# The head of a one-core hybrid trunk, taken in two halves of the channels

## The reference, cut to what matters

```python
m = jax.nn.silu(cvec) @ P['ada_w'][i] + P['ada_b'][i]
sh1, sc1, g1, sh2, sc2, g2 = jnp.split(m[:, None, :].astype(x.dtype), N_MOD, axis=-1)
h = rmsnorm(x, P['norm_mix_g'][i]) * (1 + sc1) + sh1
...
u = h @ P['ssd_w_in'][e]          # z, xBC, dt, and three parts of the short convolution
```

## Time and profile before

| | |
|---|---|
| median of 3 runs | 1944.35 us |
| the profiled execution | 1945.39 us |
| its span (first to last instruction) | 1943.7 us |
| TensorE matmul busy | 1889.1 us, 97% |
| VectorE / ScalarE / GpSimd busy | 1029.5 / 671.9 / 634.9 us |
| mean granted TensorE clock | 0.988 |
| chain that ended last | TensorE 88%, "issue" 5%, ScalarE 2%, VectorE 2%, GpSimd 1%, DMA 1% |

### The profile page before, as it was taken

The page is one execution under the profiler, slowest core; times in us unless marked ns, Lnnn a source line. Parts: engine busy times, 40 slices in busy tenths (PEclk is TensorE's granted clock), DMA queues, the critical chain, the costliest instruction groups (busy, mean ns, idle before and its releaser), DMA issues.

```text
span 1943.7 us, 35169 instructions
## 1 busy us (share of the span) xinstructions
PE 1889.1 (97%) x13400; PEld 1806.9 (93%) x13400; DVE 1029.5 (53%) x1987; ACT 671.9 (35%) x1021; POOL 634.9 (33%) x309
## 2 busy tenths in 40 slices
PE   5999999999999999999999999999999999999997
PEld 3998888888899999999999999987899999999997
DVE  5647777777714555303554354567665553035543
ACT  4443232323413443312333422147444433223332
POOL 1222222222222333443334433333223333433341
PEclk8999999999999999999999999999999999999998
DMA  8224444544543222222222432211322222222122
GB/s 323 76 75 163 155 147 135 168 154 149 177 134 105 66 76 73 65 78 76 76 63 68 140 98 84 87 42 32 96 66 67 74 73 66 80 84 73 55 68 74
DMA packets 273028, 192.48 MB, mean 99 GB/s; under 512 B 25386, under 2 KB 259238, under 8 KB 271414
## 3 DMA queue, kind: packets, MB, share of 16 engines
q1 hardware_dynamic: 267782, 182.81, 30.6%
q10 hardware_dynamic: 5168, 8.59, 1.2%
HBM read 181.31 MB, written 10.06 MB: 98 GB/s over the span
## 4 chain that ended last, share of the span: by engine, by line
PE 88%; issue 5%; ACT 2%; DVE 2%; POOL 1%; DMA 1%; SPq 0%; POOLq 0%; ACTq 0%; DVEq 0%
PE ps L618 26%; PE ps L622 25%; PE ps L619 25%; PE ps L689 2%; POOL w_lo L553 1%; PE ps L1045 1%; PE ps L866 1%; PE ps L1025 1%; PE ps L991 1%; DVE act_lo L1612 1%; ACT sp L1401 1%; PE ps L696 0%; PE ps L786 0%; DMA first<-in_ada_w 0%; PE ps L1064 0%
## 5 line engine op out<-in xcount | busy, mean ns | idle before, releaser
L553 POOL TENSOR_TENSOR w_lo<-raw,w_hi 128x1024 fp32r<-128x1024 f32 x244 | 598.7, 2456 | 1222.1 <-ACT w_hi L1098 1216.0
L618 PE MATMUL ps<-act_hi,w_hi 128*128 128x322 f32 x2752 | 846.4, 314 | 4.4 <-DVE act_lo L1612 2.6
L619 PE MATMUL ps<-act_lo,w_hi 128*128 128x322 f32 x2624 | 801.9, 312 | 0.0
L622 PE MATMUL ps<-act_hi,w_lo 128*128 128x322 f32 x2752 | 635.1, 312 | 0.0
L618 PEld LDWEIGHTS ps<-act_hi,w_hi 128*128 128x128 f32 x2752 | 524.1, 190 | 18.9 <-issue 13.0
L619 PEld LDWEIGHTS ps<-act_lo,w_hi 128*128 128x128 f32 x2624 | 497.5, 190 | 0.0
L622 PEld LDWEIGHTS ps<-act_hi,w_lo 128*128 128x128 f32 x2752 | 465.3, 189 | 0.0
L1098 ACT ACTIVATE w_hi<-raw 128x1024 fp32r<-128x1024 f32 x244 | 256.1, 1051 | 365.1 <-PE ps L622 324.2
L618 PE MATMUL ps<-f_hi,w_hi 128*128 128x322 f32 x704 | 214.2, 311 | 0.0
L619 PE MATMUL ps<-f_lo,w_hi 128*128 128x322 f32 x704 | 213.7, 310 | 0.0
L1903 DVE SCALAR_TENSOR_TENSOR x<-ps,mod,x 128x128 f32 (+1 forms) x144 | 54.4, 433 | 269.6 <-PE ps L622 269.0
(11 more groups left out here) (296 smaller groups left out, 1939.8 us busy)
## 6 DMA issues: line engine op xcount, KB each, us to landing
ada<-in_ada_w SPq DMA_DIRECT2D x40, 1024.0 KB, 5.9
raw<-in_ssd_w_in SPq DMA_DIRECT2D x44, 512.0 KB, 3.9
raw<-in_ffn_w_gate SPq DMA_DIRECT2D x44, 512.0 KB, 3.7
raw<-in_ffn_w_up SPq DMA_DIRECT2D x44, 512.0 KB, 3.8
raw<-in_ffn_w_down SPq DMA_DIRECT2D x32, 384.0 KB, 3.4
raw<-in_na_w_qkv SPq DMA_DIRECT2D x24, 512.0 KB, 3.8
raw<-in_ffn_w_down SPq DMA_DIRECT2D x32, 320.0 KB, 3.1
first<-in_ada_w SPq DMA_DIRECT2D x8, 1024.0 KB, 13.3
```

The lines of the kernel that those rows point to most:

```text
L553: g.tensor_tensor(w_lo[:, s], raw[:, s % RAW], w_hi[:, s], ALU.subtract).then_inc(S["low_split"], 1)
L618: t.matmul(out, hi, chunk_of(src_hi, k0 + k, cols), start=start, stop=False)
L619: t.matmul(out, hi, chunk_of(src_lo, k0 + k, cols), start=False, stop=False)
L622: mm = t.matmul(ps[:, 2 * tset + h, 0:HALF], lo, chunk_of(src_hi, k0 + k, cols), start=False, stop=stop)
```

## The change

SyncE loads `ada_w` as sixteen quarters of 512 KB: first for all 8 input chunks the columns of output channels 0 to 511 (shift and scale), then weight tile 0, then the same for channels 512 to 1023, into 12 quarter buffers. Behind them come weight tiles 1, `tabr`, 2 and 3, and only then x goes to DRAM. TensorE takes the first half's sums between the transposes, the second half's between the steps of chunks 0 to 2. ScalarE splits weight tile 0 ahead of its chunks and tile 1 in the middle; its exponential (with the table load) moves behind the chunks. VectorE makes `xn` chunk by chunk, the modulation half by half; `dskip` and the mask instructions move to later places.

```diff
             for n in range(2 * C):
+                if n == C:
+                    weights(SLOT_IN, 0, 0, rows(w_in, 0, C, U_BC))
+                if n >= len(quarters):
+                    sp.wait_ge(S["first_summed"], n - len(quarters) + 1)
+                src = bass.AP(tensor=ada_w.tensor, offset=(n % C) * P * MODS * D + (n // C) * ADA_N, ap=[[MODS * D, P], [D, 2], [1, ADA_N]])
+                sp.dma_start(quarters[n % len(quarters)], src).then_inc(S[f"first_loaded{n}"], 16)
+            for s in range(1, RAW):
                 weights(SLOT_IN, 0, s, rows(w_in, 0, C, U_BC + s * P))
             sp.dma_start(tabr[:], na_rpb[0]).then_inc(S["table_loaded"], 16)
+            for s in range(RAW, 4):
+                weights(SLOT_IN, 0, s, rows(w_in, 0, C, U_BC + s * P))
             sp.wait_ge(S["x_copied"], C)
             sp.dma_start(x_dram, x[:]).then_inc(S["x_spilled"], 16)
...
+            def first_sum(half, k):
+                n = half * C + k
+                pe.wait_ge(S[f"first_loaded{n}"], 16)
+                for b in range(4):
+                    cols = slice(b % 2 * 2 * P, b % 2 * 2 * P + 2 * P)
+                    mm = t.matmul(ps[ADA_COLS * b:ADA_COLS * b + ADA_COLS, 3 if half else 7, 0:2 * P], csil_w[:, k, :],
+                                  quarters[n % len(quarters)][:, b // 2, cols], start=(k == 0), stop=(k == C - 1))
+                mm.then_inc(S["first_summed"], 1)
+            def first_turn(half):
+                pe.wait_ge(S["first_copied"], half + 1)
...              # two matmuls, where line 724 had four
             for s in range(C):
...              # transposes as before
+                first_sum(0, s)
             norm_spread(0)
+            first_turn(0)
             pe.wait_ge(S["x_copied"], C)
             pe.wait_ge(S["wdt_ready"], 1)
-            pe.wait_ge(S["mod_ready"], 1)
             for k in range(C):
+                if k == 1:
+                    pe.wait_ge(S["rinv_ready"], 1)
                 pe.wait_ge(S["act_ready"], k + 1)
+                if k == C // 2:
+                    pe.wait_ge(S["mod_ready"], 1)
...              # dt matmuls
                 mm = half_slot(0, 0, [k], act_hi, act_lo, k == 0, k == C - 1)
+                for n in ((0, 1, 2), (3, 4, 5), (6, 7), ())[k] if k < 4 else ():
+                    first_sum(1, n)
+                if k == C // 2 - 1:
+                    first_turn(1)
...
             a(wdt_hi[:], wdt[:], ACT.Copy).then_inc(S["wdt_high"], 1)
+            act.wait_ge(S["first_summed"], C)
+            a(arow[:, 0:2 * P], ps[:, 7, 0:2 * P], ACT.Copy).then_inc(S["first_copied"], 1)
             inverse(0)
-            a(dtb[:, 1, :], dtb[:, 1, :], ACT.Exp).then_inc(S["a_exp"], 1)
-            a(arow[:], ps[:, 7, :], ACT.Copy).then_inc(S["first_copied"], 1)
+            split(SLOT_IN, 0, 0)
             for c in range(C):
+                if c == C // 2:
+                    act.wait_ge(S["first_summed"], 2 * C)
+                    a(arow[:, 2 * P:4 * P], ps[:, 3, 0:2 * P], ACT.Copy).then_inc(S["first_copied"], 1)
+                    for s in range(1, RAW):
+                        split(SLOT_IN, 0, s)
+                if c % (C // 2) == 0:
+                    act.wait_ge(S["half_ready"], c // (C // 2) + 1)
...              # act_hi, nt as before, each also behind x_scaled
-                if c < RAW:
-                    split(SLOT_IN, 0, c)
+            act.wait_ge(S["dskip_loaded"], 48)
+            a(dtb[:, 1, :], dtb[:, 1, :], ACT.Exp).then_inc(S["a_exp"], 1)
             for s in range(RAW, 4):
                 split(SLOT_IN, 0, s)
...
-            for c0 in range(C):
-                tt(xn[:, c0 * T:c0 * T + T], x[:, c0 * T:c0 * T + T], rinv[:], ALU.mult).then_inc(S["x_scaled"], 1)
...              # dskip, masks: moved to later places
+            def half_modulation(half):
+                dve.wait_ge(S["first_turned"], half + 1)
...              # mod (scale), scale_a, mod (shift) for 4 chunks
+                dve.sem_inc(S["half_ready"], 1)
+            scaled_x(0)
             for c in range(C):
+                if c == C // 2:
+                    for later in range(c + 1, C):
+                        scaled_x(later)
+                if c % (C // 2) == 0:
+                    half_modulation(c // (C // 2))
                 if c % 2 == 0:
...              # nt
+                    if c < C // 2:
+                        scaled_x(c + 1)
                     st.wait()
                 else:
+                    if c < C // 2:
+                        scaled_x(c + 1)
                     dve.wait_ge(S["nt_ready"], c // 2 + 1)
                 dve.wait_ge(S["act_high"], c + 1)
                 tt(act_lo[:, c * T:c * T + T], nt[:, c % 2], act_hi[:, c * T:c * T + T], ALU.subtract).then_inc(S["act_ready"], 1)
...
             new_sum()
+            # dskip: two instructions, here, ahead of tab
...
             st.did(tt(sc[:, :, K_END, :], sc[:, :, K_END, :], sc[:, :, K_DT, :], ALU.mult))
+            # the masks: some 20 small instructions, here (old line 1716)
```

More of the change, by code:

```diff
@@ L217, in trunk @@
         first = [at(f"first{n}", o, [P, 4, ADA_N]) for n, o in enumerate(first_at)]
-        first += [nc.alloc_sbuf_tensor_at(f"first{5 + n}", [P, 4, ADA_N], F32, offset=first_lo_at + n * 2 * C * P * 4) for n in range(2)]
+        first += [nc.alloc_sbuf_tensor_at("first5", [P, 4, ADA_N], F32, offset=first_lo_at + 2 * C * P * 4)]
+        quarters = [f[:, 2 * q:2 * q + 2, :] for f in first for q in range(2)]
         xs = at("xs", 0, [P, C * T])
@@ L380, in _ @@
                 params(R_FW[lay], ffn_conv_w[lay].rearrange(k_p, p=P))
[L381 to L386, removed]
+            for n in range(2 * C):
+                if n == C:
[5 more added lines that the diff above has]
+            for s in range(1, RAW):
                 weights(SLOT_IN, 0, s, rows(w_in, 0, C, U_BC + s * P))
             sp.dma_start(tabr[:], na_rpb[0]).then_inc(S["table_loaded"], 16)
+            for s in range(RAW, 4):
+                weights(SLOT_IN, 0, s, rows(w_in, 0, C, U_BC + s * P))
             sp.wait_ge(S["x_copied"], C)
             sp.dma_start(x_dram, x[:]).then_inc(S["x_spilled"], 16)
-            for s in range(RAW, 4):
-                weights(SLOT_IN, 0, s, rows(w_in, 0, C, U_BC + s * P))
             with sp.Fori(0, 2) as i:
@@ L706, in _ @@
             pe.wait_ge(S["tokens_loaded"], 32)
+            def first_sum(half, k):
[8 more added lines that the diff above has]
+                pe.wait_ge(S["first_copied"], half + 1)
+                picks = ident[:].rearrange("p (b q) -> p b q", b=4)[:, :, 0:2]
+                for n in range(2):
+                    mm = t.matmul(ps[:, 4, 16 * half + 8 * n:16 * half + 8 * n + 8], arow[:, (2 * half + n) * P:(2 * half + n) * P + P], picks,
+                                  start=True, stop=True)
+                mm.then_inc(S["first_turned"], 1)
             for s in range(C):
@@ L1192, in _ @@
                         act.wait_ge(S["act_ready"], c)
+                    act.wait_ge(S["x_scaled"], c + 2)
                     for lo, hi, stream in STREAMS:
@@ L1558, in inverse @@
                 v.reciprocal(rinv_t, root_t).then_inc(S["token_inverse"], 1)
[L1560 to L1572, removed]
-            for c in range(C):
+            def half_modulation(half):
+                dve.wait_ge(S["first_turned"], half + 1)
+                turned = ps[:, 4, 16 * half:16 * half + 16].rearrange("p (n m h s) -> p m h n s", n=2, m=2, h=2)
+                at_ = slice(C // 2 * half, C // 2 * half + C // 2)
+                for m in (1, 0):
+                    adab = par[:, R_ADAB + m * C:R_ADAB + m * C + C][:, at_].rearrange("p (h n) -> p h n", h=2).unsqueeze(3).broadcast_to([P, 2, 2, 2])
+                    ins = tt(mod[:, m, at_].rearrange("p (h n) s -> p h n s", h=2), turned[:, m], adab, ALU.add)
+                    if m == 1:
+                        st.then_wait(ins)
+                        st.did(stt(scale_a[:, at_], mod[:, 1, at_], 1.0, bcast(par[:, R_NMIX:R_NMIX + C][:, at_], 2, [P, C // 2, 2]), ALU.add, ALU.mult))
+                if half == 1:
+                    dve.sem_inc(S["scale_ready"], 1)
+                    ins.then_inc(S["mod_ready"], 1)
+                    dve.wait_ge(S["mod_ready"], 1)
+                else:
+                    st.did(ins)
+                st.wait()
+                dve.sem_inc(S["half_ready"], 1)
@@ L1574, in _, with scaled_x @@
+            def scaled_x(c):
+                tt(xn[:, c * T:c * T + T], x[:, c * T:c * T + T], rinv[:], ALU.mult).then_inc(S["x_scaled"], 1)
+            scaled_x(0)
+            for c in range(C):
+                if c == C // 2:
[3 more added lines that the diff above has]
+                    half_modulation(c // (C // 2))
                 if c % 2 == 0:
@@ L1576, in _ @@
                         dve.wait_ge(S["act_ready"], c - 1)
+                    dve.wait_ge(S["x_scaled"], c + 1)
                     for lo, hi, stream in STREAMS:
```

(21 more changed lines are left out.)

9 lines of the change are left out of this document (3 added, 6 removed).

## The result

The median of 18 runs of the changed kernel is 1948.17 us (1943.14 to 1952.78), of 18 runs of the kernel before beside it 1944.9 us (1941.01 to 1946.66): ratio 1.0017 [1.001, 1.0024], +3.3 us. Forecast were 1944.9, with 1941.8 to 1948.3 as range and "within 0.2%" as the likeliest case. The direction of the small shift, its mechanism and its place came out; its size was 0.5 us in the forecast and is 1.6 us where it was forecast, and in the medians some 1.5 to 2 us more come behind that place. The profiled execution took 1950.83 (span 1949.1, mean granted clock 0.988).

The account below looks back on a forecast made before the run. TensorE, 97% busy, was taken to bound the kernel, with tile 3 held by the convolution chain. The head's gains are given back, leaving +0.5 us: 1945.39 to 1945.9 profiled, median 1944.35 to 1944.9; range 1941.8 to 1948.3.

Parts of the forecast that it names:

- Landing of the first half: DMA of the first eight quarters (4.2 MB, 2 KB rows): 11 us, the last quarter landing at about 23.2.
- Rival D: First half lands late, 25.5 at 0.33 MB/us; chunk 0 1.3 us later, second half late too: 1947.6; chance 0.18.
- 13.99 + 2.5 x (1.07 + 0.9) + 5.5 x (0.55 + 0.45) = 24.4: TensorE's end of first-half transposes and sums: 2.5 chunks at the slow pace, 5.5 at the fast one.
- Clock behind the idle stretch: TensorE, idle from 25.6 to 32.1, starts chunk 0 at 1.2 GHz; chunk 0 takes 3.22 us.
- Rival B: TensorE keeps 2.4 GHz after its idle stretch or rises soon: -1.8 us, 1942.6; chance 0.14.
- Table load: ScalarE's 1.28 us load for the exponential stands behind chunk 7, near 54; no further drain counted.
- rival C: Table load stands ahead of chunk 0, hidden by the lock; -1.28 us from the forecast, 1943.6; chance 0.10.
- The wait ahead of tile 3: TensorE stands 2.4 us until ScalarE's gpad copy frees tile 3's set; tile 3 starts at about 75.5, +0.5 us.
- Rival E: Tile 3 doesn't wait for the convolution chain, so TensorE's 1.9 us come through: 1942.4; chance 0.08.
- Behind tile 3 the same program follows, so the +0.5 stays: From tile 3 on nothing changes, with dt's sums (6 us) as slack for ScalarE; +0.5 us remains to the end.
- its case of over 3.9 us: Whole kernel slower by over 3.9 us, by very slow landing or a 1.7 us clock fall ahead of tile 3; chance 0.11.
- x_spill and the masks, at nothing: Later x_spill costs 0; masks moved into VectorE's 5.06 us idle ahead of 98.21 cost 0, up to 1 under the lock.

Follow-up runs that it names:

- e4: Kernel before with only its exponential and table load moved behind the chunks: 1946.85 us, 1.0002 of the kernel before.
- e2: Changed kernel with the memset and 15 tab copies moved behind the first four convolutions: 1946.55 us, 1.0002 of the kernel before.
- e5: Kernel before with the tab copies moved behind the first four convolutions: 1945.32 us, 0.9995 of the kernel before.
- e6: Changed kernel with 13 extra matmuls into an unused bank, filling TensorE's wait ahead of tile 3: 1950.72 us, 1.0024 of the kernel before.
- e7: Changed kernel with exponential early, tab copies late, tile 1's split ahead of the wait for the second half's sums: 1946.43 us, 0.9998 of the kernel before.
- e10: Changed kernel with four second-half sums ahead of chunk 0, the last four behind chunks 0 and 1, the turn behind chunk 2: 1948.02 us.
- e1: Changed kernel with the exponential and its table load put back ahead of arow: 1947.13 us, 1.0007 of the kernel before.
- e12: Changed kernel with four sums ahead of chunk 0, exponential and tile 1's split early, dskip and tab behind the convolutions: 3 us above the expected 1940.5.
- e14: Changed kernel with dt's 50 small matmuls spread, ten behind each of tile 4's first five chunks: 1944.90 us, 0.9992 of the kernel before.

## Why the prediction was right, and by which steps it was short

**Landing of the first half: right.** The last quarter landed at 23.4 (forecast 23.2), and the last four came 1.4 us apart, so some 0.38 MB/us for rows of 2 KB, near the rates of the wider rows. Rival D had the right sign and nearly the right time (1947.6), for the wrong cause. Its own working does not come out either: 4.2 MB at 0.33 MB/us from the same start are over at 24.9, not 25.5.

**"13.99 + 2.5 x (1.07 + 0.9) + 5.5 x (0.55 + 0.45) = 24.4": the mis-sized term.** The sums ended at 26.8. A chunk took 2.27 us at the low pace and 1.27 at the high one (20.43 to 21.70 in the rows above), not 1.97 and 1.00: a half sum takes 0.58 us, not 0.45, which had been divided out of a sum of twice the width, and the five transposes 0.69, not 0.55. Eight chunks make 2.4 us. (The two levels are read from the pace, which changed near 19.8; the profile's granted clock stands at 1.00 from 12 us on.) ScalarE's split of tile 0 slid with it (28.04), so the lock closed later too and the first `scale_a` slipped in (0.17 us), against the forecast's sign of two long ones; the lock met `nt` instead (2.55 us for a pair that was put at 0.8). Chunk 0 came at 33.68, 1.6 us later than forecast, and each step behind it is late by a little less: the end of chunk 7 by 1.3 (59.65), dt's chain by 1.1, which at 63.95 is past the sign's 62 to 63.5, and tile 3 by 1.2.

**Clock behind the idle stretch: right.** Chunk 0 ran at 1.2 GHz until about 37:

```profile
33.70:37.00 3.30, 3.30 (x12) 2.49 (x12) 2.35 (x5) 2.51 (x5) 0.00 (x0) 0.50 1.12 335
```

Rival B is out. **Table load: right.** At 55.44, behind the chunks (forecast near 54), and the next activation at 56.73, straight behind its 1.28 us. No load stands between `rinv` and chunk 0's Identity in this trace, so rival C is out. The Trainium skill ("ScalarE: Activation LUTs", section "What ACT_TABLE_LOAD costs") states a further drain of some 1380 ns for every switch to a different set; this trace, like the one before, shows none. The Trainium skill (same page, section "Table sets: the hidden batching unit") has identity in every set; for the set of the root, this trace agrees.

**The wait ahead of tile 3: right.** 2.19 us for 2.4, by `gpad`, along the chain named, though TensorE and the chain both came over 1 us later than forecast. e4 makes it in the kernel before, e2 takes it away; e5 shows the chain had slack before. Rival E is out.

**"Behind tile 3 the same program follows, so the +0.5 stays": failed.** The program is the same, its clock is not. The prediction had named a further fall of the clock during the wait, at 1.7 us, but only in its case of over 3.9 us; the sum has it at nothing. It happened, in both profiles of the changed kernel: 0.50 from 78.1 to 81.3, and tile 3 took 1.6 us more. The second fall, within the sums, was not named at all. It is there in each of the eleven profiles, of either kernel, in which the small matmuls stand in one stretch, and in none of the three in which they are spread. But its length is not tied to the change: it is 3.4 us in the one profile of the kernel before, 6.8 in e2, e5, e6, e7 and e10, and 10.2 in both profiles of the kernel after, e1, e4 and e12. e4 and e5 are kernels without halves, and e5, e7 and e12 have no wait ahead of tile 3. So neither the halves nor the wait is needed for a long fall, and what sets its length stays open, and with it the cause of the 1.5 to 2 us that the medians have over the 1.6. The spread of 3.2 us also stays in e14 (2.9), so it is not from this stretch alone.

**x_spill and the masks, at nothing: nothing in the trace against it,** though neither was tried alone. `x_spill` landed at 59.3, tile 4's load was issued at 60.56 and took 3.6 us, as such loads do (3.8). The masks stand from 94.98 to 98.9 (21 instructions of VectorE; the 19 and 2.9 us of the prediction are the count of a window, and before they took 33.07 to 36.99), and no wait of TensorE follows them up to 130.

## What to carry to other kernels

Work that a first engine does sooner is only worth what the next shared resource lets through: here 7 us won up to chunk 0 came back as sums, as a wait in the middle, and at tile 3 as a loss, for which one table load of 1.28 us that moved onto the path of another chain is enough by itself (e4). Where one engine's work locks out another's, list the small instructions in the order in which the lock meets them; moving one away (e1) brings the next under it. Spreading the run of very small matmuls between large ones gave some 2.9 us to the kernel before and some 5 to the kernel after, where the change itself costs 3.3. A gain of 3 us at one place of a profile need not be in the median (e6), and a difference of 0.2% is only read from many runs beside their granted clocks.

## What the runs showed of the hardware that was not expected

- A load on the other queue landed much sooner beside smaller rows: that of `wdt`, issued at 1.8 us in both kernels, took 23.7 us to land beside rows of 8 KB and 13.7 beside rows of 2 KB; `dld` 25.4 and 11.3. So it is in every profile: `wdt` 23.2 to 24.2 us in the four with rows of 8 KB, 13.6 to 14.7 in the ten with 2 KB. Landing rows of `wdt`, before and after:

```profile
DMA to landing us min/median/max: 23.7/23.7/23.7
```

```profile
DMA to landing us min/median/max: 13.7/13.7/13.7
```

- VectorE gets one or two instructions in between two of GpSimd's splits (the second `dskip` of e1 stood 2.35 us again behind the first's 1.80; of `tab`'s copies the first stood 1.87, the second ran in 0.16, the third stood 2.37), and a small one that reads SBUF stands for the whole split otherwise: `dskip` 4.16 us against 0.34, `scale_a` 1.36 against 0.17, while `mod`, from PSUM, kept to 0.16 in the middle of the lock (29.19 in e7).
- TensorE at its faster pace needed 1.27 us for four 128-column transposes, another one and a sum of eight matmuls with 32 stationary columns, where the forecast had put them together from the earlier trace rows as 1.0.
